# The down projections of a two-layer feed-forward stage as seven quadrant products instead of eight blocks

## The reference, cut to what matters

```python
D_FF = 2816
def conv_ffn(h, w_up, conv_w, conv_b, w_down):
    up = h @ w_up                                  # 512 x 1024 by 1024 x 5632
    a, bval = up[..., :D_FF], up[..., D_FF:]
    a = causal_conv_3(a, conv_w) + conv_b
    return (silu(a) * bval) @ w_down               # 512 x 2816 by 2816 x 1024
...
    h = rms_norm(x, norm_ffn[l])
    x = x + conv_ffn(h, w_up[l], conv_w[l], conv_b[l], w_down[l])
...
return rms_norm(x, norm_final)
```

## Time and profile before

| | us |
|---|---|
| median of three runs | 2156.01 |
| the profiled execution, its own time | 2156.16 |
| its span, first to last instruction | 2154.3 |
| TensorE busy in the span | 2129.8 (99%), 10315 matmuls |
| TensorE weight loads | 1757.6 (82%) |
| VectorE busy | 1276.6 (59%) |
| ScalarE busy | 781.4 (36%) |
| GpSimd busy | 26.6 (1%) |
| DMA, over the span | 217.73 MB, mean 101 GB/s |

### The profile page before, as it was taken

One profiled execution on the slowest core, in us unless ns is written; L12 is line 12 of the kernel. 1 busy time (PEld: TensorE's weight loads), 2 busy tenths in 40 slices (PEclk: granted clock), 3 DMA queues, 4 the chain that ended last, 5 costly groups with the idle time before them and its releaser, 6 DMA issues.

```text
span 2154.3 us, 24865 instructions
## 1 busy us (share of the span) xinstructions
PE 2129.8 (99%) x10315; PEld 1757.6 (82%) x10315; DVE 1276.6 (59%) x1649; ACT 781.4 (36%) x1036; POOL 26.6 (1%) x41
## 2 busy tenths in 40 slices
PE   7999999999999999999999999999999999999998
PEld 4888888888888887888888888888788888888887
DVE  6899897953665848535665554234853566555422
ACT  3323232223343344444343333135444434333312
POOL 1000000000000100000000000000000000000000
PEclk9999999999999999999999999999999999999999
DMA  9432232233332322322223233223231222323222
GB/s 315 146 118 84 98 103 83 98 117 98 98 93 95 111 79 79 130 67 94 83 84 113 79 109 103 91 69 98 79 137 61 97 78 91 105 83 113 99 88 78
DMA packets 181588, 217.73 MB, mean 101 GB/s; under 512 B 3932, under 2 KB 153316, under 8 KB 181220
## 3 DMA queue, kind: packets, MB, share of 16 engines
q1 hardware_dynamic: 178080, 209.47, 29.5%
q10 hardware_dynamic: 2948, 4.52, 0.6%
q0 software_dynamic: 448, 2.15, 0.3%
HBM read 211.93 MB, written 4.19 MB: 100 GB/s over the span
## 4 chain that ended last, share of the span: by engine, by line
PE 94%; DVE 4%; issue 1%; DMA 1%; ACT 1%; POOL 0%; SPq 0%; POOLq 0%; ACTq 0%; DVEq 0%
PE psum L1812 30%; PE psum L1813 30%; PE psum L1814 30%; DVE whl L504 1%; PE psum L2225 1%; DMA ada<-in_w_ada 1%; PE psum L2257 1%; PE psum L2237 1%; PE psum L2180 0%; PE psum L2210 0%; PE psum L2196 0%; PE psum L1836 0%; PE psum L1955 0%; DVE mrow L1686 0%; POOL stat L668 0%
## 5 line engine op out<-in xcount | busy, mean ns | idle before, releaser
L1812 PE MATMUL psum<-hT,whl 128*128 128x512 f32 (+1 forms) x2064 | 789.1, 382 | 2.8 <-DVE whl L504 1.5
L1814 PE MATMUL psum<-hT,whl 128*128 128x512 f32 (+1 forms) x2064 | 783.1, 379 | 0.0
L1813 PE MATMUL psum<-hT,whl 128*128 128x512 f32 (+1 forms) x2064 | 783.0, 379 | 0.0
L504 DVE TENSOR_TENSOR whl<-raw,whl 128x1024 fp32r<-128x1024 f32 x361 | 438.5, 1217 | 419.5 <-ACT whl L497 419.3
L497 ACT ACTIVATE whl<-raw 128x1024 fp32r<-128x1024 f32 x361 | 376.8, 1047 | 421.3 <-PE psum L1814 386.8
L1812 PEld LDWEIGHTS psum<-hT,whl 128*128 128x128 f32 x2064 | 388.1, 188 | 83.4 <-issue 6.7
L1814 PEld LDWEIGHTS psum<-hT,whl 128*128 128x128 f32 x2064 | 388.2, 188 | 73.7
L1813 PEld LDWEIGHTS psum<-hT,whl 128*128 128x128 f32 x2064 | 388.3, 188 | 71.2 <-issue 0.2
L1812 PE MATMUL psum<-whl,ff 128*128 128x512 f32 x352 | 137.1, 389 | 0.0
L1814 PE MATMUL psum<-whl,ff 128*128 128x512 f32 x352 | 136.9, 389 | 0.0
L1813 PE MATMUL psum<-whl,ff 128*128 128x512 f32 x352 | 136.9, 389 | 0.0
(11 more groups left out here) (309 smaller groups left out, 2106.9 us busy)
## 6 DMA issues: line engine op xcount, KB each, us to landing
raw<-in_w_in SPq DMA_DIRECT2D x87, 1024.0 KB, 5.1
raw<-in_w_up SPq DMA_DIRECT2D x44, 1024.0 KB, 5.1
raw<-in_w_down SPq DMA_DIRECT2D x20, 1024.0 KB, 5.0
raw<-in_w_branch SPq DMA_DIRECT2D x12, 1024.0 KB, 5.1
raw<-in_w_out SPq DMA_DIRECT2D x12, 1024.0 KB, 5.0
ada<-in_w_ada SPq DMA_DIRECT2D x8, 1024.0 KB, 9.7
ada<-in_w_ada SPq DMA_DIRECT2D x8, 512.0 KB, 11.1
x<-in_x SPq DMA_DIRECT2D x4, 512.0 KB, 5.6
```

What stands on the lines that cost most here:

```text
L504: nc.vector.tensor_tensor(whl_view(w, 1), raw_view(w), whl_view(w, 0).bitcast(F), ALU.subtract).then_inc(w_lo, 1)
L1812: M(out_, stat_hi, mov_hi, start=start, stop=False, **kw)
L1813: M(out_, stat_hi, mov_lo, start=False, stop=False, **kw)
L1814: return M(out_, stat_lo, mov_hi, start=False, stop=stop, **kw)
```

## The change

The 2 x 2 quadrants are: tokens 0 to 255 and 256 to 511, the first and the second k tile of each of the eleven pairs, and columns 0 to 511 and 512 to 1023. With A the activation and B the weight, the form computed is

S1 = A21 + A22, S2 = S1 - A11, S4 = A12 - S2, S3 = A11 - A21; T1 = B12 - B11, T4 = B22 - B21 - T1, T3 = B22 - B12, T2 = B11 + T3;
P1 = A11 B11, P2 = A12 B21, P3 = S4 B22, P4 = A22 T4, P5 = S1 T1, P6 = S2 T2, P7 = S3 T3.

P1 and P2 of pair kk share the piece sA (B11, B21), P4 and P5 share sB (T4, T1), P6 and P3 share sC (T2, B22), P7 has pieces sD. PE runs three passes: sA and sB of all eleven pairs, then sC of all pairs, then sD: 11 x 7 x 2 token blocks x 3 = 462 matmuls a layer. P6 is accumulated onto P1's banks and P7 onto both, with DVE adding the banks to `x` in between (16 adds of 512 columns a layer instead of 8).

The token sums S1 (kept in place of A21 + A22 in `ff`), S2, S4 and S3 are made by DVE at the end of each f2 of the up projection, S2 to S3 are split in hi and lo into a staging tile that lies on `x`, and POOL stores each pair's 0.79 MB to DRAM; ACT's queue brings them back over `ff` when sA and sB of the pair are used. So that the tiles fit, `x` (2.1 MB) is itself stored to DRAM at the start of the up projection and loaded back by POOL after the last sums are stored. A third weight buffer, the tiles of T1 and T4, and the first three T3 lie on `hT`. The weight sums T1, T4, T3 and T2 are all made by DVE. The core of the diff:

```diff
-        rows("w_down_2", l, FT)
+        for kk in range(PAIRS):
+            add("w_down_2", ("quad", l, kk), [("sA", l, kk), ("sB", l, kk)], 1024)
+        for i in range(0, PAIRS, 2):
+            add("w_down_2", ("diag", l, i), [("sC", l, k) for k in range(i, min(i + 2, PAIRS))], 1024)
+        for j, ks in enumerate(T3_PAIRS):          # ((0, 1), (2,), (3, 4), (5, 6), (7, 8), (9, 10))
+            number[("sD", l, j)] = len(number)
+            chunks[-1][2].append((("sD", l, j), 512 * len(ks)))
...
+            def raw_released(c):
+                held = chunks[c][1]
+                if held[0] == "quad":
+                    sp.wait_ge(t_sum, PAIRS * held[1] + held[2] + 1)
+                    sp.wait_ge(t3_done, PAIRS * held[1] + held[2] + 1)
...
+                if key[0] == "quad" and key[2] == 2:
+                    sp.wait_ge(w_used, W[("up_b", key[1], FT - 1)] + 1)
...
+            def down_sums(l):                      # POOL
+                pool.wait_ge(x_ready, 4 * (1 + 2 * l) + 4)
+                pool.dma_start(x_dram[l], x[:]...).then_inc(x_moved, 16)
+                for kk in range(PAIRS):
+                    pool.wait_ge(s_lo, PAIRS * l + kk + 1)
+                    pool.dma_start(s_dram[l, kk], sstage[:]...).then_inc(s_stored, 16)
+                pool.wait_ge(s_stored, 16 * PAIRS * (l + 1))
+                pool.wait_ge(w_lo, W[("sB", l, 0)] + 1)
+                pool.dma_start(x[:]..., x_dram[l]).then_inc(x_moved, 16)
...
+                def sums_back(kk):                 # ACT
+                    act.wait_ge(w_used, W[("sB", l, kk)] + 1)
+                    act.wait_ge(s_stored, 16 * (PAIRS * l + kk + 1))
+                    if kk >= 2:
+                        act.wait_ge(s_back[kk % 2], back_count(l, kk - 2))
+                    act.dma_start(ff_r[:, kk, 0:1536].bitcast(F), s_dram[l, kk]).then_inc(s_back[kk % 2], 16)
+                for w in range(W[("sA", l, 0)], W[("sD", l, 0)] + 1):
+                    split_hi(w + 3)
+                    if key_of[w][0] == "sA" and key_of[w][2]:
+                        sums_back(key_of[w][2] - 1)
+                    if key_of[w] == ("sC", l, 0):
+                        sums_back(PAIRS - 1)
...
+            def t1_and_t4(l, kk):                  # DVE
+                dve.wait_ge(raw_in[RAW_BUF[c]], RAW_NEED[c])
+                link(V.tensor_tensor(tsum_of(kk), q[:, :, 1, :], q[:, :, 0, :], ALU.subtract))
+                V.tensor_tensor(tsum_of(kk)[:, 1, :], tsum_of(kk)[:, 1, :], tsum_of(kk)[:, 0, :], ALU.subtract).then_inc(t_sum, 1)
...
+                for w in range(W[("sA", l, 0)], W[("sC", l, PAIRS - 1)] + 1):     # DVE, quad_rows
+                    ahead = key_of[w + 3]
+                    if ahead == ("sB", l, 1):
+                        t1_and_t4(l, 1)
+                    if ahead[0] == "sB" and ahead[2] < PAIRS - 1:
+                        t1_and_t4(l, ahead[2] + 1)
+                    if ahead == ("sB", l, PAIRS - 1):
+                        t2(l, 0)
+                    if ahead[0] == "sC" and ahead[2] < PAIRS - 1:
+                        t2(l, ahead[2] + 1)
+                    split_lo(w + 3)
+                    if ahead == ("sB", l, 1):
+                        t3(0)
+                        t3(1)
+                    elif ahead[0] == "sA":
+                        t3(ahead[2])
...
+                gained(s, 0)                       # layer 0, behind the splits of sD
+                norm_lo(s, 0)
+                gained(s, 1)
+                whole_row(2)                       # two adds, then x_ready
+                statistics(2)
+                norm_lo(s, 1)
+                split_lo(w0 + 4)
+                whole_row(3)
+                split_lo(w0 + 5)
...
+                    await_read(dve, ("up_b", l, 2 * f2 + 1))                      # DVE, end of each f2
+                    V.tensor_tensor(fsil[:, 0, 256:], fsil[:, 0, 256:], fsil[:, 1, 256:], ALU.add).then_inc(s_sums, 1)
+                    if f2 == PAIRS - 1:
+                        split_lo(W[("up_b", l, FT - 1)] + 3)
+                    link(V.tensor_tensor(ssum[:, 0:256], fsil[:, 0, 256:], fsil[:, 0, 0:256], ALU.subtract))
+                    V.tensor_tensor(ssum[:, 256:768]..., fsil[:, 1, :]..., ssum[:, 0:256]..., ALU.subtract).then_inc(s_sums, 1)
...
+                    dve.wait_ge(s_hi, PAIRS * l + f2 + 1)
+                    V.tensor_tensor(sstage[:, 1, :], ssum[:], sstage[:, 0, :].bitcast(F), ALU.subtract).then_inc(s_lo, 1)
...
+                for i in range(2):                 # PE, last pass of quad_tiles
+                    for j in range(2, 6):
+                        ins = seventh(j, i)
...
+                    if s < STAGES - 1:
+                        if i == 0:
+                            transposed(s, 0)
+                            transposed(s, 1)
+                        else:
+                            transposed(s, 2)
```

More of the change, by code:

```diff
@@ L174, in build @@
     NP_ = len(pieces)
+    key_of = list(W)
+    RAW_BUF, RAW_NEED, RAW_PREV = [], [], []
+    loads, holder = [0, 0, 0], [None, None, None]
+    other = 0
+    for c, (_, key, _) in enumerate(chunks):
+        if key[0] == "quad":
+            b = other if key[2] % 3 == 0 else 1 - other if key[2] % 3 == 1 else 2
+        elif key[0] == "diag":
+            b = (2, other, 1 - other)[key[2] // 2 % 3]
+        else:
+            b = other
+        RAW_BUF.append(b)
+        RAW_PREV.append(holder[b])
+        holder[b] = c
+        loads[b] += 2 if key[0] == "diag" else 1
+        RAW_NEED.append(16 * loads[b])
+        if key[0] not in ("quad", "diag"):
+            other = 1 - b
     W_BANK = {}
@@ L508, in build @@
         ROWS = [("w_out", None, KT)] + [s for l in range(LAYERS) for s in (("w_out_2", l, KT), ("w_down_2", l, FT))]
+        PLAIN = [stage for stage in ROWS if stage[0] != "w_down_2"]
         def resident(stage):
             name, l, nk = stage
-            return W[(name, l, 1, nk - 8)]
+            return W[("sD", l, 2)] if name == "w_down_2" else W[(name, l, 1, nk - 8)]
         def lead_keys(stage):
@@ L540, in row_wait @@
             elif tb < 3:
-                eng.wait_ge(row_full, ROWS.index(stage) * 6 + half * 3 + tb + 1)
+                eng.wait_ge(row_full, PLAIN.index(stage) * 6 + half * 3 + tb + 1)
             else:
@@ L545, in row_reads, with back_count @@
         def row_reads(stage, half, tb):
-            i = ROWS.index(stage)
+            i = PLAIN.index(stage)
             return 2 * tb + half + 1 if i == 0 else 8 + 4 * (i - 1) + tb + 1
+        def back_count(l, kk):
+            return 16 * (l * len(range(kk % 2, PAIRS, 2)) + kk // 2 + 1)
         def proj_wait(eng, s_full, name, l, j, mm):
@@ L902, in norm, with first_square @@
                 norm_hi(s, 3)
+            def first_square(tb):
+                act.wait_ge(quad_read, 12 * (LAYERS - 1) + (5 + tb if tb < 2 else 9 + tb))
+                if tb:
+                    act.wait_ge(s_sq0, tb)
+                A(xn2[:, 0, 0:512], x[:, tb, 0:512], ACT.Square, accum_out=ssq0[:, tb:tb + 1]).then_inc(s_sq0, 1)
             for l in range(LAYERS):
@@ L1057, in _ @@
                     for j in range(2):
[L1058 to L1063, removed]
+                        split_hi(W[("up_b", l, 2 * f2 + j)] + 3)
+                    act.wait_ge(s_sums, 2 * (PAIRS * l + f2) + 1)
+                    for j in range(2):
+                        A(ff[:, 2 * f2 + j, 0, :], fsil[:, j, :], ACT.Copy).then_inc(ff_hi, 1)
@@ L1068, in _ @@
[L1068 to L1073, removed]
+                    first_square(tb)
@@ L1551, in add_rows @@
                 s = 2 + ROWS.index(stage)
-                last = s == STAGES - 1
                 w0 = resident(stage)
```

317 lines of the change are left out of this document (286 added, 31 removed).

## The result

The changed kernel takes **2162.03 us** (median of 8 runs, 2160.95 to 2163.85) against 2155.99 before (8 runs, 2155.59 to 2156.08): ratio 1.0029, 95% interval 1.0018 to 1.0040. It is slower by 0.3%, 3.8 us over the forecast. The profiled execution took 2160.95 with a span of 2159.1, so the trace has 4.79 us more than that of before (2156.16) to explain; it is the fastest of the eight, 1.1 us under their median.

The account below looks back on a forecast made before the run. PE's count of matmuls sets the time: -29.9 + 2 x (2.5 + 6.5 + 0.3) + 1.2 + 8.1 + 1.5 + 2.7 = +2.2 us on 2156.16, so 2158.4, adjusted by 0.15 to 2158.2 us; range 2146 to 2171.

Parts of the forecast that it names:

- sB1's split: Start of down stage: ready at 10.6 us behind DVE's backlog, wanted by PE at 8.16; 2.5 us of waiting a layer.
- quads 4 to 10: First pass: quad 4 costs another 0.3 us a layer; loads up to quad 10, needed by about 57.5 us, cost nothing.
- the wait before sD: Before the third pass: PE waits for DVE's add of the banks, 0.6 us a layer, 1.2 in all.
- the tail: End of layer 0's down stage: PE waits for row 2's norm chain and following splits; 8.1 us, ends 4 and 10.
- the forecast's own range: Whole run: 2152.5 to 2163.5 us, from the ends of quad 3's wait and the tail's.
- The landing time of quad 3: Early down stage: 8.0 us, between 5.0 alone and 9.5 shared with both returns; PE waits 6.5 a layer for sB2.
- The clock: After the 6.5 us wait: clock falls 4.9 us after PE idles, slowing the first matmuls; 2.7 us in both layers.
- The end: After the last matmul: a second add (0.6) and the gain multiply (0.7 plus 0.2) lengthen the chain by 1.5 us.
- The loads don't collide: Rival, early down stage: quad 3 lands in 5.0 us, wait 3.5, clock stays up; 2149.5 us, chance 0.22.
- DMA binds the first pass: Rival, first pass: DMA below 364 GB/s, quad 10 comes 5.8 us late in each layer; 2169.8 us, chance 0.17.
- The clock stays down: Rival, behind the long wait: half clock for two pieces, 5.4 us a layer, +8.1; 2166.3 us, chance 0.08.
- the count does not fall: Rival, whole kernel: matmul count does not fall, or their distance rises with the strided products; 2183 us, chance 0.02.

Follow-up runs that it names:

- run 8: Changed kernel with POOL's return of x waiting for sB4 and the returns of the sums starting at pair 5; 2148.97 us, ratio 0.9969.
- run 4: Changed kernel with DVE doing row 2's adds right behind the gain of row 0 in layer 0's tail; 2160.15 us, ratio 1.0018.
- run 1: Changed kernel with POOL's return of x also waiting for sB4, some 20 us later in each down stage; 2156.78 us, ratio 1.0003.
- run 6: Changed kernel with the new DVE and ACT order at the down stage's start, as in run 5, but its own tail; 2141.52 us, ratio 0.9938.
- run 9: Run 7 with ACT making row 1's high half before row 2's scaling at layer 0's end; 2132.55 us, ratio 0.9891.
- run 5: Changed kernel with early T3, splits ahead of T1 and late low halves at the down stage's start, plus run 4's tail; 2139.26 us, ratio 0.9921.
- run 7: Run 5 with ACT's returns of the sums later, six at pairs 5 to 10 and five in the second pass; 2134.00 us, ratio 0.9898.

## Why the prediction came out as it did

*Right.* The up stages cost nothing; sB1's split came at 1338.30, 9.3 us in, and was done at 10.5 (10.6 predicted); quad 3 was issued 11.2 us in (11.3 predicted, though that is one T3 behind sB1's split and not the two that the text counts); then the load of quad 3 at DVE's head, with sB2's split queued behind it; quads 4 to 10 free; the wait before sD (1.2 for 1.2); the tail through row 2's chain and sv0's split (2.85 and 1.85 for 3.4 and 2.5). "What the products save the waits eat" held. The time lies inside the forecast's own range, but above its bound of 2160.3, on the side called slower, which had 0.38 against 0.40 for same.

*The landing time of quad 3* was off: "I take 8.0, nearer to the shared end", and it took 10.2, over even that end of 9.5. The step behind it is "1.05 + 0.79 + 1.05 MB move in 7.2", that is equal shares. The queues' lines above show otherwise: the sums and `x` moved first, and then `x` got four bytes for each of quad 3's, so all 2.1 MB of `x` were through before quad 3, and not half of them. The row that the prediction took for "two queues at once" (371) does not show sharing either. In its window SP's transfer moves until 900 and POOL's, issued 0.7 us behind it, only from then on; the queues' lines of the kernel before, from 897 to 900 and from 900 to 902:

```profile
q1 hardware_dynamic: 975, 0.99, 96.8%
q0 software_dynamic: 6, 0.05, 4.7%
...
q0 software_dynamic: 96, 0.79, 98.2%
q1 hardware_dynamic: 35, 0.03, 4.4%
```

The other end was real: 4.9 alone, in run 8. In PE's wait the miss of 2.2 comes to only 0.8 us a layer (14.6 for 13.0 in both), in layer 0 because PE itself came to sB2 later, through the half clock ahead of it.

*The clock* is the term furthest off: 2.7 for 6.3 in the first passes (0.7 of that stands without any wait), and 2.4 more in the tail. The row of before showed a fall some 4.9 us after PE's last matmul, and I took that for shorter waits to be free. Here 2.21 us were enough in layer 0, and in both layers of runs 4 and 8; in layer 1, and in run 1's layer 0, the same 2.21 were not, nor were 2.42 in layer 0 of run 6. The Trainium skill ("TensorE: Matmul & The Clock Gate", Part 1: the HAM clock gate) calls the number of slow matmuls variable from run to run. The spread of the times fits that without showing it: the changed kernel's runs spread over 2.9 us and run 1's over 3.8, those of run 9, without long waits, over 0.5, and those of before over 1.0 (27 runs). Part of the 6.3 is not extra, as run 1 showed: slow matmuls ahead of a wait shorten it.

*The tail* came out near its 8.1 by luck: its waits were shorter than predicted, and half clock, which the sum put at nothing there, filled the gap.

*The end* cost 0.9, not 1.5: the square of the row's first half starts at 2152.70, before the two adds end at 2153.26.

*The rivals.* "The loads don't collide" was priced within 0.5 of run 8, which is that case, but not for its reasons: its wait of 3.5 was 1.4 there, and the clock that it kept up fell in both layers. "DMA binds the first pass" was wrong for this kernel, and became true in run 5. "The clock stays down" for two pieces behind the long wait did not come: in layer 0 it was back within 4.4 us of the wait's end, less than one piece at half speed. That the count does not fall is out: run 7's pass takes 0.228 us a matmul (its price of 2183 is not worked out; the sum without the saving gives 2188).

*Left open.* Why quad 3 moved nothing until 1344, though it was issued at 1340.21, is not shown; alone, in run 8, it moved from 1341 on. What decides whether a wait of 2.21 us is followed by half clock was not tried by itself. Nor were the sums' return and `x` moved one without the other in both ways: `x` alone was (run 1), the sums alone, with the changed kernel's start, were not.

## What to carry to other kernels

When work is cut from the engine that binds, its feeders start each stage with what the engine used to give them time for: look at their backlog at the stage's first microseconds, not at their busy share. Issue first whatever frees a load buffer, then whatever feeds the next piece, and last what nobody waits for within the stage. And put transfers that nobody needs yet (here the sums and `x`) where DMA is idle: the sums, moved later, were worth 5 us in run 7, and the sums and `x` together, with the buffers freed late, 13 in run 8.

## What was unexpected of the hardware

- Half clock with a wait of only 2.21 us: some 1.5 us after the matmuls had resumed in layer 0 of the changed kernel, 0.3 before they did in layer 1 of run 8, and not at all in other stages. The remainder of the pass, 0.35 without a wait (run 7), was 0.6 to 4.4 us with waits, with no visible tie to their length (2.2 behind the single wait of 2.55 in run 5, 1.9 behind 10.13 in the changed kernel).
- DMA moved 421 GB/s over 4 us with several queues holding work, 419 over 3 with SP's alone, and 380 over 60 (run 5). The Trainium skill ("DMA: Bandwidth & Descriptors", Specifications) gives about 358 GB/s as a core's limit for HBM, half of what the two cores of a stack share; with one core running the measurements lie above it, and they decide.
- One transfer of 1 MB landed 4.9, 7.2 or 10.2 us after its issue by its company alone, and the return of `x` (2 MB by POOL) 14.0 in run 5, 11.0 in run 7.
- From 1344 to 1347 POOL's queue and SP's got 63 and 59 packets, but 1.03 and 0.24 MB: with both moving, the queue with the larger packets got the bytes.
